# Modulation slabs from GpSimd's queue, and retention gates as seven-product units

## The reference, cut to what matters

```python
m_lat = split(cond_lat @ mod_w[layer] + mod_b[layer], 6)     # same for the context
h_lat = modulate(rms_norm(x, norm_g[layer, 0]), m_lat[0], m_lat[1])

p  = split_parts(h_lat @ w_in, q=1024, k=1024, v=2048, g=2048)   # w_in: 1024 x 6144
pc = project_parts(h_ctx, w_in, ['k', 'v'])                      # last layer: k, v only
q, k = apply_rope(heads(p.q)), apply_rope(heads(p.k)) * 1/16
o = retention(q, k, v, decays, state of the context)
y = (rms_norm(o) * silu(p.g)) @ w_out
x = x + m_lat[2] * y
```

## Time and profile before

| | |
|---|---|
| median of three runs | 2650.14 us |
| profiled execution | 2651.96 us, span of the records 2650.1 us |
| TensorE busy | 2554.4 us, 96% of the span; granted clock 0.997 |
| VectorE busy | 1540.6 us, 58% |
| ScalarE busy | 646.5 us, 24% |
| GpSimd busy | 0.2 us |
| DMA | 386.6 MB, 146 GB/s over the span |

### The profile page before, as it was taken

How to read it: one execution, slowest core, us unless ns; L and a number is a source line. 1 busy time by engine, 2 the same in 40 slices (tenths; PEclk the granted TensorE clock), 3 DMA queues, 4 the chain that set the end, 5 groups by cost and what they waited for, 6 DMA issues and landing times.

```text
span 2650.1 us, 38697 instructions
## 1 busy us (share of the span) xinstructions
PE 2554.4 (96%) x15804; PEld 1938.7 (73%) x15804; DVE 1540.6 (58%) x3021; ACT 646.5 (24%) x1709; POOL 0.2 (0%) x4
## 2 busy tenths in 40 slices
PE   6999899999999999999999999999999999999999
PEld 2545557888887864599996845659997855667999
DVE  4866667655876543266664664426773764434785
ACT  3144412111002111222202152233321144232320
POOL 0000000000000000000000000000000000000000
PEclk9999999999999999999999999999999999999999
DMA  8531115555574684245643432125663433114563
GB/s 331 198 94 46 43 32 175 153 179 161 202 274 162 259 302 167 80 128 160 191 164 127 159 64 96 65 96 150 169 190 134 147 107 96 65 65 142 164 178 123
DMA packets 335212, 386.62 MB, mean 146 GB/s; under 512 B 11052, under 2 KB 264124, under 8 KB 322748
## 3 DMA queue, kind: packets, MB, share of 16 engines
q1 hardware_dynamic: 332300, 378.15, 44.3%
q10 hardware_dynamic: 2736, 6.01, 0.6%
HBM read 383.08 MB, written 1.05 MB: 145 GB/s over the span
## 4 chain that ended last, share of the span: by engine, by line
PE 75%; DVE 11%; DMA 6%; issue 4%; ACT 3%; SPq 1%; ACTq 0%; DVEq 0%
PE acc L864 27%; PE acc L915 12%; PE mx L864 11%; PE acc L903 7%; PE acc L929 6%; DMA mod_w<-in_w_ada 2%; DVE arena L2516 2%; DMA mod_w<-in_mod_w 2%; PE acc L1233 2%; PE acc L1284 2%; PE mx L1632 1%; DVE arena L3358 1%; PE mx L1094 1%; DVE hT L2549 1%; PE mx L1619 1%
## 5 line engine op out<-in xcount | busy, mean ns | idle before, releaser
L864 PE MATMUL acc<-arena 128*128 128x128 f32 (+1 forms) x2248 | 360.9, 303 | 3.4 <-DVE arena L3104 1.0
L864 PEld LDWEIGHTS acc<-arena 128*128 128x128 f32 x2248 | 314.1, 191 | 22.1 <-ACT gate L2186 1.4
L915 PE MATMUL acc<-hT,ring 128*128 128x256 f32 (+1 forms) x1280 | 305.5, 401 | 2.2 <-ACT hT L1847 1.3
L915 PEld LDWEIGHTS acc<-hT,ring 128*128 128x128 f32 x1280 | 242.5, 190 | 63.3 <-issue 32.1
L2516 DVE SCALAR_TENSOR_TENSOR arena<-mod_w,vcols,arena 128x2048 f32<-128x2048 f32 x98 | 228.4, 2348 | 74.6 <-DMA mod_w<-in_w_ada 59.2
L903 PE MATMUL acc<-ring,hT 128*128 128x512 f32 x576 | 251.1, 596 | 6.4 <-DMA ring<-in_even_w_in 4.2
L929 PE MATMUL acc<-ring,hT 128*128 128x512 f32 x512 | 247.6, 605 | 0.7 <-ACT hT L1969 0.7
L903 PEld LDWEIGHTS acc<-ring,hT 128*128 128x128 f32 x576 | 109.3, 191 | 144.8 <-issue 136.2
L2880 DVE TENSOR_TENSOR arena<-ring 128x512 f32<-128x512 f32 (+1 forms) x136 | 91.7, 674 | 194.1 <-PE acc L864 182.0
L864 PE MATMUL acc<-hT,ring 128*128 128x128 f32 (+1 forms) x1272 | 194.8, 303 | 4.6 <-ACT hT L1937 2.2
L864 PE MATMUL acc<-arena,ring 128*128 128x128 f32 (+1 forms) x1224 | 190.7, 299 | 4.7 <-DVE arena L3006 2.4
(11 more groups left out here) (433 smaller groups left out, 3344.9 us busy)
## 6 DMA issues: line engine op xcount, KB each, us to landing
ring<-in_w_in SPq DMA_DIRECT2D x28, 2048.0 KB
mod_w<-in_w_ada SPq DMA_DIRECT2D x48, 1024.0 KB, 5.0
ring<-in_ffn_w_in SPq DMA_DIRECT2D x88, 512.0 KB
ring<-in_w_up SPq DMA_DIRECT2D x88, 512.0 KB
mod_w<-in_mod_w SPq DMA_DIRECT2D x40, 1024.0 KB, 4.9
ring<-in_odd_w_in SPq DMA_DIRECT2D x12, 2048.0 KB
ring<-in_ffn_w_out SPq DMA_DIRECT2D x16, 1024.0 KB
ring<-in_w_down SPq DMA_DIRECT2D x16, 1024.0 KB
```

Of the source, the lines that this page charges most:

```text
L864: ins = nc.tensor.matmul(out, w[:, k, :], h[:, k, :], start=start and k == 0, stop=stop and k == n - 1, skip_group_check=more)
L915: ins = nc.tensor.matmul(b[:, 0:hi - lo], w[:, k, P * f:P * (f + 1)], hT[:, k, lo:hi], start=k == 0, stop=k == KD - 1)
```

## The change

1. SP issues weight tiles alone. The slabs are issued by GpSimd, in a block of their own: each waits only for `mod_used` (and the first and the seventeenth for the region to be free).
2. The gates leave `by_token` and become four more units of `retention_values`, tiles 4 to 7, each for the latent pair alone. So the order of tiles is values, gates, queries, keys. The intermediate results land in the gates' place raw, and ACT applies Silu there after the keys (8 instructions), signalled by one more count on `rv_c01`, on which the first `weighted` waits.
3. The input sums of the latent pair move into the buffer `gate`, so ACT issues the first two decay tables after the units.
4. Slabs: units take 0, 2 x 7, then 1 x 4; the remaining 10 are used in one piece ahead of the rotations, where 8, 2, 2, 2 stood among them. The sums after jobs 19 and 30 move to 20 and 26.

```diff
-MOD_SUM_AFTER = {"even": (13,), "odd": (4, 8, 19, 30)}
+MOD_SUM_AFTER = {"even": (13,), "odd": (4, 8, 20, 26)}
 MOD_EARLY = 8
 MOD_UP_SUM, MOD_DOWN_SUM = {9: 3, 19: 4}, {3: 5, 7: 6, 11: 7}
-MOD_UNITS, MOD_ODD = (0, 2, 2, 2, 2, 2, 2, 2), (8, 2, 2, 2)
+MOD_UNITS, MOD_ODD = (0, 2, 2, 2, 2, 2, 2, 2, 1, 1, 1, 1), 10
...
+RV_UNITS = [(c, pair) for c in range(4) for pair in range(2)] + [(c, 1) for c in range(4, 8)]
+
+
+def rv_last(c):
+
+    return max(q for q in range(len(RV_UNITS)) if RV_UNITS[q][0] == c) + 1
...
     a.start("ret_v")
-    for c in range(4):
-        a.ring_used("unit", 2 * c + 2, 2)
-    tiles("odd", (("ret_q", [4, 4]), ("ret_k", [4, 4]), ("ret_g", [2] * 4)))
-    a.slab_tile += [a.tile["ret_v"] + n for n in (2, 2, 2, 2, 4, 4, 4, 4, 6, 6, 6, 6, 8, 8, 8, 8, 8, 10, 10, 10, 10, 10,
-                                                  12, 12, 14, 14, 16, 16)]
+    for c in range(8):
+        a.ring_used("unit", rv_last(c), 2)
+    tiles("odd", (("ret_q", [4, 4]), ("ret_k", [4, 4])))
...
-            return [view(8192 + 2048 * pair + 512 * j, 4, P) for j in range(4)]
+            if pair == 0:
+                return [view(8192 + 512 * j, 4, P) for j in range(4)]
+            return [gate[:, j // 2, 512 * (j % 2):512 * (j % 2) + 512].rearrange("p (k n) -> p k n", k=4) for j in range(4)]
...
-            return rv[:, 2 * (q % 2) + i, 512 * (q // 2) + 256 * t:512 * (q // 2) + 256 * t + 256]
+            c, pair = RV_UNITS[q]
+            at = 512 * (c % 4) + 256 * t
+            return rv[:, 2 * pair + i, at:at + 256] if c < 4 else rg[:, i, at:at + 256]
...
-            def load_slabs(t):
-
-                while slab.n < len(pl.slab_tile):
-                    i = slab.n
-                    if i in first_tile and t < first_tile[i]:
-                        return
-                    if i >= 2 and pl.slab_tile[i - 2] > t - 2 * RING:
-                        return
-                    if i >= 2:
-                        sp.wait_ge(mod_used, i - 1)
-                    layer, g = MOD_GROUPS[1 + i // KD]
-                    w = a["mod_w"][layer] if layer < 2 else a["w_ada_2"][layer - 2]
-                    k = i % KD
-                    sp.dma_start(mod_w[:, i % 2, :], w[P * k:P * (k + 1), 2048 * g:2048 * g + 2048]).then_inc(
-                        mod_in[i % 2], 16)
-                    slab.next()
...
-            for c in (4, 5, 6, 7, 0, 1, 2, 3, 8, 9, 10, 11):
+            for c in (4, 5, 6, 7, 8, 9, 10, 11, 0, 1, 2, 3):
...
+        @block.gpsimd
+        def _(pool):
+            for i in range(KD * (len(MOD_GROUPS) - 1)):
+                if i == 0:
+                    pool.wait_ge(w_part, pl.released[pl.tile["even_bi"] - 2 * RING][1])
+                elif i == 2 * KD:
+                    pool.wait_ge(acc_full, pl.released[pl.tile["ffn0"] - 1][1])
+                if i >= 2:
+                    pool.wait_ge(mod_used, i - 1)
+                layer, g = MOD_GROUPS[1 + i // KD]
+                w = a["mod_w"][layer] if layer < 2 else a["w_ada_2"][layer - 2]
+                k = i % KD
+                pool.dma_start(mod_w[:, i % 2, :], w[P * k:P * (k + 1), 2048 * g:2048 * g + 2048]).then_inc(mod_in[i % 2], 16)
...
-                units = 8
+                units = len(RV_UNITS)
...
-                    if q % 2 == 0:
+                    if RV_UNITS[q][0] not in B:
                         first = tile.n
                         weights(512)
-                        B[q // 2] = rv_tile(first)
+                        B[RV_UNITS[q][0]] = rv_tile(first)
...
-            for _ in range(4):
-                by_token(LAT, 512, where="odd")
...
-            table(0)
-            table(1)
             own.n = 0
             p1, u2, u3 = (rv_copies[:, j] for j in range(3))
-            for q in range(9):
+            units = len(RV_UNITS)
+            for q in range(units + 1):
...
+            table(0)
+            table(1)
...
+                act.wait_ge(rv_c10, 9 + c)
                 for t in range(2):
-                    evac(rg[:, t, 512 * c:512 * (c + 1)], 512, ACT.Silu)
-                    mod_after("odd")
+                    g = rg[:, t, 512 * c:512 * (c + 1)]
+                    ins = nc.scalar.activation(g, g, ACT.Silu)
+            ins.then_inc(rv_c01, 1)
...
-                    need(dve, rv_z, 2 * c - 2)
+                    if c >= 2:
+                        dve.wait_ge(rv_z, rv_last(c - 2))
...
-                if q % 2 == 1 and q < 7:
-                    value_weights_summed(q // 2 + 1)
-                if q < 8:
+                if q < units - 1 and RV_UNITS[q + 1][0] > RV_UNITS[q][0]:
+                    value_weights_summed(RV_UNITS[q + 1][0])
+                if q < units:
...
+            mod_slabs(MOD_ODD)
             for h in range(RET):
-                mod_slabs(MOD_ODD[h])
...
-            job_done("ret_g", 8)
+            dve.wait_ge(rv_c01, len(RV_UNITS) + 1)
```

More of the change, by code:

```diff
@@ L325, in make_plan @@
     a.weights("even_out", [KD], "V")
-    first = a.tile["even_q"]
-    a.slab_tile = [first] * 4 + [first + 2] * 6 + [first + 4] * 4 + [first + 8] * 2
     a.free_jobs("norm1", 1)
     a.sevens("ffn0", "down0")
-    a.slab_tile += [a.tile["ffn0"] + q - 1 for q in range(KF) for _ in range(up_slabs(q))]
-    a.slab_tile += [a.tile["down0"] + n for n in range(4 * len(CHUNKS)) for _ in range(DOWN_SLABS[n])]
     a.free_jobs("norm2", 1)
     a.start("ret_v")
-    for c in range(4):
-        a.ring_used("unit", 2 * c + 2, 2)
-    tiles("odd", (("ret_q", [4, 4]), ("ret_k", [4, 4]), ("ret_g", [2] * 4)))
-    a.slab_tile += [a.tile["ret_v"] + n for n in (2, 2, 2, 2, 4, 4, 4, 4, 6, 6, 6, 6, 8, 8, 8, 8, 8, 10, 10, 10, 10, 10,
-                                                  12, 12, 14, 14, 16, 16)]
+    for c in range(8):
+        a.ring_used("unit", rv_last(c), 2)
+    tiles("odd", (("ret_q", [4, 4]), ("ret_k", [4, 4])))
     a.free_jobs("ret_oT", KD)
@@ L824, in _ @@
                 down_chunks(a["w_down_2"][l])
-            assert tile.n == pl.tiles and slab.n == len(pl.slab_tile)
+            assert tile.n == pl.tiles
             for p in range(4):
@@ L1543, in product2 @@
                     need(pe, rv_c00, q)
-                    product(seven(5, 256), A[q % 2][0][1], B[q // 2][1][0], True, True,
+                    product(seven(5, 256), A[RV_UNITS[q][1]][0][1], B[RV_UNITS[q][0]][1][0], True, True,
                             (lambda k: pe.wait_ge(h_ready, KD * use + KD // 2 + k + 1)) if q == 0
@@ L1548, in product5 @@
                 def product5(q):
-                    pe.wait_ge(rv_t, 4 * (q // 2) + 2)
+                    pe.wait_ge(rv_t, 4 * RV_UNITS[q][0] + 2)
                     if q < 2:
@@ L1560, in product6 @@
                     pe.wait_ge(rv_p1s, q + 1)
-                    product(x_(q), rv_sums(q % 2)[2], rv_weight_sums(q // 2)[1], False, True, more=True).then_inc(rv_p6, 1)
+                    product(x_(q), rv_sums(RV_UNITS[q][1])[2], rv_weight_sums(RV_UNITS[q][0])[1], False, True, more=True).then_inc(rv_p6, 1)
                 def product7(q):
                     pe.wait_ge(rv_u2s, q + 1)
-                    product(x_(q), rv_sums(q % 2)[1], rv_weight_sums(q // 2)[0], False, True, more=True).then_inc(rv_p7, 1)
+                    product(x_(q), rv_sums(RV_UNITS[q][1])[1], rv_weight_sums(RV_UNITS[q][0])[0], False, True, more=True).then_inc(rv_p7, 1)
                 def product4(q):
@@ L3127, in _ @@
             p1, u2, u3 = (rv_copies[:, j] for j in range(3))
-            for q in range(10):
-                if 1 <= q < 9:
+            units = len(RV_UNITS)
+            for q in range(units + 2):
+                if 1 <= q < units + 1:
                     o = q - 1
```

22 lines of the change are left out of this document (8 added, 14 removed).

## The result

The changed kernel takes 2660.71 us (median of five runs, 2659.87 to 2661.35), the kernel before 2650.14. The ratio is 1.0038, 95% interval 1.0026 to 1.0050: slower by 0.38%. The forecast was 2653, range 2643 to 2661. The time lies 0.3 us inside the range's upper end, in rival B's place (2658 and over), not in the forecast's. "Slower by over 0.2%" had been given a chance of 0.35.

What follows compares the result with a forecast made beforehand. TensorE, busy 96% of the span, was taken as the bound. Terms -6.6 - 5.3 + 8.5 + 2.1 + 1.5 + 2.5 = +2.7 us gave 2652.8 against the median, forecast 2653, range 2643 to 2661.

Steps and rivals of the forecast that it cites:

- rival B: Gate units: tile and slab together need 10.5 us or more; slabs late elsewhere too; +8.2 us, 2658; chance 0.35 with Rival D.
- step 5: Down stage: a chunk's third slab, issued by GpSimd, lands in about 6.3 us; +1.5 us, bounds -1 and +4.
- the prediction's own sign: Whole kernel: the forecast is wrong if the time is under 2647 or over 2658 us.
- the stretch that it put at about 248 us: From 829.84 to the first scores at 1080.89: 251.05 us in the kernel before, about 248 expected.
- Term 6: First projection: GpSimd's first two slabs share transfer with TensorE's weight tile and delay it; +2.5 us, bounds -1.5 and +5.
- Step 1: Gates: four units of seven products at 1.727 us replace 128 records at 0.4292 us; -6.6 us of TensorE work.
- Step 2: Value units: slabs out of SP's queue remove waits for slabs and c11; -5.3 us, bounds -4 and -5.7.
- Step 3: Gate units: tiles turned over in one unit land late, beside a slab; +8.5 us, bounds 4.2 and 11.
- Step 4: Keys to scores: without gates between, the first weighting waits for the last head's rotation and Silus; +2.1 us, bounds 1.5 and 3.
- Step 6: First projection: its start, 40.81 before, delayed by GpSimd's slabs beside the weight tile; +2.5 us, bounds -1.5 and +5.
- Rival D: GpSimd's slab issue: VectorE's double-rate TENSOR_SCALAR delays it by up to 1.24 us; +2 on the forecast, chance small, inside rival B.

Runs made afterwards that it cites:

- e4: The changed kernel with the gate units' products reordered, the older tile's last reader first, so the next tile's load is issued 3.5 us earlier; 2649.08 us, 0.9997.
- e1: The kernel before with only its slabs issued by GpSimd, gates by token as before; 2651.68 us, 1.0007.
- r1: No edit: second profile of both the kernel before and the changed kernel; mixer stretch of the changed kernel 250.99 us.
- e3: The changed kernel with no slab used in the four gate units, their four slabs coming after them; 2654.95 us, 1.0017.
- e5: The changed kernel with two slabs used in each gate unit instead of one, 6 after them instead of 10; 2675.17 us, 1.0092.
- e7: e4 with ACT's eight Silus placed between the keys' copies and each head's query rotated without waiting for its key; 2646.83 us, 0.9988.
- e6: e4 with SP issuing the first 60 slabs, each ahead of its tile, and GpSimd only the odd mixer's 28; 2643.90 us, 0.9975.
- e2: The changed kernel with SP issuing the slabs again, each ahead of a weight tile; 2664.22 us, 1.0051.
- e8: The changed kernel with the edits of e4, e6 and e7 together; 2641.65 us, 0.9968.
- r2: No edit: third profile of both the kernel before and the changed kernel; mixer stretch of the changed kernel 253.95 us.

## Why the forecast was wrong in size, step by step

But for a part of step 5 the mechanisms were the right ones, and the sum failed in two terms and in one place that it didn't contain. By the prediction's own sign (wrong over 2658) it missed, and the stretch that it put at about 248 us took 252.7 in the mean. Its terms measured -6.6, -4.8, +12.7, +1.6, +5.9 and about 0, and +4.2 lay outside of it: +13.0, where the means of the profiles differ by 12.8 and the forecast was +2.7. Term 6, put some 2.5 us too high, covered part of what the others lacked, and that much of the nearness is luck.

- **Step 1**, -6.6 for the products: holds. Every product without a wait takes 1.727 us in the gate units too, and e4, which has no waits left there, is 5.7 us under e1 in the mixer stretch, with a wait of 1.16 us for a query tile on the other side.
- **Step 2**, -5.3 for the value units: measured -4.8 (e1). I had counted as a loss of the slabs a wait of 0.47 us for ACT's copy that e1 has too: its 49 products take 86.98 us and not my 86.0.
- **Step 3**, +8.5, bounds 4.2 and 11: the term was mis-sized. It measured 12.7 us in the profile (12.1 without ACT's copy), and the stretch is 12.5 longer than e4's. The landing of 10.5 to 10.8 us was my upper bound, where I had taken a middle value. The slab is issued within 1.6 us of the tile in the second and third transition, in all three profiles, since VectorE ends its slab just when product4 is done, so the sharing is no matter of chance. And 3.45 us of it in this profile are a term that I didn't have, TensorE's lower clock after waits of 2.5 and 3.6 us; without it the loss is 9.2, inside my bounds, as are the 9.7 of r1, where the clock held. The low end stood on a tile in 7.3 us, which has no row; the fastest in the gate units took 7.9 (e3). That the loss follows the bytes beside the tile is shown by e3 and e5, that the late release of the slot is its root by e4.
- **Step 4**, +2.1: measured +1.6, removed by e7. (5 x 8.65 us of slabs is 43 and not 45, which changes nothing.)
- **Step 5**, +1.5, bounds -1 and +4: the term was mis-sized, and its mechanism was incomplete. The first feed forward lost 5.9 us in the mean of three, 4.6 up to 790 in e1. I had priced only a slower landing of the third slab. Of that there is little (5.3 us against 5.0 over all slabs). What I had not seen is that SP's single queue did something useful there: it put slabs ahead of tiles, and the queue of its own lets a tile start first, so TensorE waits at one more place and longer at the two others, and at the last the wait of 2.12 us was followed by the lower clock (1.7 us). e6 undoes it. The Trainium skill's turn-taking between queues, packet by packet (DMA: Bandwidth & Descriptors, "Queues, rings and completion order"), which I weighed only for the gate units, agrees with this place as well: the slab issued 0.2 us after the tile had VectorE wait 3.28 us.
- **Step 6**, +2.5: not seen. The first projection starts at 40.59 in the changed kernel's profile and 40.81 in that of the kernel before; the means of three differ by 0.6, and the even mixer is not to be told from no change. Over all fourteen profiles the first projection starts at 41.7 in the mean where GpSimd issues the first slabs (eight, 40.4 to 42.6) and at 40.8 where SP does (six, 40.3 to 42.1), so about 1 us may be real; they overlap too much to call it shown.
- **Not in the sum**: +4.2 between the scores and 1325, of which 0.6 lie between the scores and 1320 and 3.6 at one tile near 1320 (in two of the changed kernel's three profiles the lower clock follows that wait too); and a wait for the second query tile, 0.63, 1.42 and 2.48 us in the changed kernel's three profiles.

Rival B had the right place, tiles of 10.5 us, and a near total (+8.2). It had 11 for term 3 and 4 for term 5, both nearer than the forecast's, and was wrong in term 6; it knew nothing of the 4.2 us after the scores, so its total is near in part by luck.

Rival D (VectorE holding up GpSimd's issue) exists and costs next to nothing. One of the 88 issues falls on VectorE's TENSOR_SCALAR, and takes 1.25 us instead of 0.53, until 0.13 us after that operation's end:

```profile
798.92 1.28 DVE L2513 TENSOR_SCALAR arena<-mod_w,vcols 128x2048 f32<-128x2048 f32 x1
799.08 1.25 POOL L829 DMA_DIRECT2D mod_w<-in_w_ada  x1 [10.50 <-DVE arena L2515]
```

So it is in each of the eight profiles in which GpSimd issues all slabs, once in each, while the issues that fall on the other form (L2515), some 30, take 0.53. This agrees with the rule of the Trainium skill that the prediction names (SBUF — State Buffer, "SBUF: two separate sides"). The price here is 0.7 us on one slab, and TensorE has no wait of over 0.5 us there.

Open is what makes the tile near 1320 late. It goes with the gates as units (ten of ten profiles; the kernel before, its repeats and e1 are on the other side), not with GpSimd's slabs (e2, e6 and e8 show it); the small loads ahead of it move at under 30 GB/s for 1 to 2 us longer. Why, no run tells.

## What to carry to other kernels

A weight tile that serves one unit instead of two turns the slot's last reader into the critical step: see first whether that product can stand earlier in the unit (e4: some 11 us for an order of seven products), before counting what the arithmetic saves. In these runs transfers competed by bytes and by order, whichever engine issued them; moving a stream to its own queue takes away waits in the old queue but also the order that this queue kept, so do it stage by stage (e6) and check in each who used to go first. When a profile holds one example of the shared case and one of the lone case, take the shared one as the value, not as the bound.

## What the runs showed of the hardware that was not expected

- A wait of TensorE of over 2 us is often followed by some 8 records of 256 columns (11 to 13 in e2 and e5) at 0.427 us instead of 0.216 (granted clock 0.52 in 962.5 to 966.0, that is 1.2 GHz instead of 2.4). In the changed kernel's first profile this added 3.45 us to waits of 9.2 in the gate units and 1.7 us to one of 2.1 in the down stage. It is not certain: r2 of the same kernel shows it after waits of 2.2 and 3.0 us in the gate units, but in r1 waits of 2.2 and 3.3 us there had no slow record behind them, and the mixer stretch took 250.99 us instead of 253.10. The shortest wait of the value, gate and down stages with slow records behind it is 1.89 us (e1, at 788.89).
- A slab of 1 MB issued by GpSimd lands in 5.3 us in the median, by SP in 5.0; 86 of the 88 issues cost GpSimd 0.53 us each. The one that falls on VectorE's TENSOR_SCALAR (f32, 2048 columns, 1.28 us) takes 1.25.
- A 2 MB tile lands in 7.9 us alone, 10.2 to 10.8 with a slab of 1 MB issued from the other queue up to 1.6 us after it, 12.2 to 12.8 with two such slabs (e5), and 9.5 to 9.8 behind a slab in the same queue (10.2 from the slab's issue).
